# Gathering rows in quarters, a router by tile pairs and own banks for the first expert, in a hybrid encoder layer

## The reference

```
h      = rmsnorm(x1) * ffn_norm_g
logits = h @ w_router + b_router                  # 512 x 32
top 4 of 32 experts per token, softmax over the four -> gates
for each (token, expert) chosen:
    hu  = h @ w_gate_up[e] + b_gate_up[e]         # 1024 x 2048
    a   = min(hu[:1024], 7);  lin = clip(hu[1024:], -7, 7)
    act = a * sigmoid(1.702 a) * (lin + 1)
    y  += gate * (act @ w_down[e] + b_down[e])    # 1024 x 1024
out = rmsnorm(x1 + y) * final_norm_g
```

## Time and profile before

| | |
|---|---|
| three runs | 1348.56, 1343.34, 1342.54 us; median 1343.34 |
| profiled execution | 1343.47 us, span 1341.6 |
| PE busy | 1303.3 us (97%) |
| DVE / ACT / POOL busy | 508.4 / 205.2 / 246.7 us |
| bytes moved by DMA | 450.76 MB, mean 336 GB/s |
| mean granted TensorE clock | 0.988 |

### The profile page before, as it was taken

The page is one execution under the profiler, slowest core; times in us unless marked ns, Lnnn a source line. Parts: engine busy times, 40 slices in busy tenths (PEclk is TensorE's granted clock), DMA queues, the critical chain, the costliest instruction groups (busy, mean ns, idle before and its releaser), DMA issues.

```text
span 1341.6 us, 33185 instructions
## 1 busy us (share of the span) xinstructions
PE 1303.3 (97%) x14022; PEld 640.3 (48%) x14022; DVE 508.4 (38%) x895; ACT 205.2 (15%) x316; POOL 246.7 (18%) x252
## 2 busy tenths in 40 slices
PE   6999999998999999999999999999999999999996
PEld 6767778853444444444444444444444344444343
DVE  7676635542333332333222222222233333332235
ACT  5243333310010000001000000000010000000002
POOL 2145434100222211111111111111111111111100
PEclk9999998989999999999999999999999999999998
DMA  9222114678999999999999999999999999999984
GB/s 264 78 80 65 40 62 162 270 278 338 385 406 401 400 397 403 405 410 401 400 407 408 399 399 410 408 410 407 408 407 404 406 407 406 406 403 400 411 345 145
DMA packets 94606, 450.76 MB, mean 336 GB/s; under 512 B 12105, under 2 KB 36953, under 8 KB 45424
## 3 DMA queue, kind: packets, MB, share of 16 engines
q1 hardware_dynamic: 83280, 426.27, 79.6%
q0 software_dynamic: 8656, 19.48, 5.9%
q10 hardware_dynamic: 2640, 4.59, 0.9%
HBM read 440.06 MB, written 18.67 MB: 342 GB/s over the span
## 4 chain that ended last, share of the span: by engine, by line
PE 80%; DMA 9%; DVE 4%; SPq 3%; issue 2%; POOL 1%; ACT 1%; DVEq 0%; POOLq 0%; ACTq 0%
PE gu_bank L1630 40%; PE bank L1644 21%; DMA raw<-in_w_gate_up_dram 9%; PE bank L1391 4%; PE bank L1393 4%; PE bank L1392 4%; SPq L400 3%; PE bank L1618 2%; PE bank L1468 1%; PE bank L1482 1%; PE bank L1445 1%; PE bank L1647 1%; PE bank L1605 1%; DMA x_sb<-in_x_dram 0%; PE bank L1402 0%
## 5 line engine op out<-in xcount | busy, mean ns | idle before, releaser
L1630 PE MATMUL gu_bank<-raw,xT 128*32 128x512 f32 x3072 | 337.5, 592 | 4.7 <-DMA raw<-in_w_gate_up_dram 4.7
L1287 DVE TENSOR_TENSOR gate_in<-gu_bank,b_gu 128x768 f32<-128x768 f32 x32 | 30.6, 957 | 555.0 <-PE gu_bank L1630 542.0
L1630 PEld LDWEIGHTS gu_bank<-raw,xT 128*32 128x32 f32 x3072 | 100.5, 110 | 234.2 <-issue 211.9
L1644 PE MATMUL bank<-raw_a,aT 128*32 128x256 f32 x2232 | 166.8, 380 | 0.0
L1647 PE MATMUL bank<-raw_a,aT 128*32 128x256 f32 x744 | 166.4, 380 | 0.0
L1630 PE MATMUL gu_bank<-raw_c,xT 128*32 128x512 f32 x1488 | 165.5, 592 | 0.0
L589 POOL DMA_INDIRECT sum_rows<-y_out,scatter_list x31 | 45.6, 1472 | 418.0 <-ACT y_out L878 401.7
L1312 DVE STREAM_TRANSPOSE aT<-lin_in 128x192 f32<-128x192 f32 x128 | 68.0, 533 | 143.2 <-PE bank L1647 142.1
L1644 PEld LDWEIGHTS bank<-raw_a,aT 128*32 128x32 f32 x2232 | 88.8, 110 | 62.0
L864 ACT ACTIVATE xT<-bank 128x384 f32<-128x384 f32 x66 | 28.9, 489 | 551.9 <-PE bank L1618 541.4
L1630 PEld LDWEIGHTS gu_bank<-raw_c,xT 128*32 128x32 f32 x1488 | 49.8, 110 | 109.8 <-issue 103.5
(11 more groups left out here) (252 smaller groups left out, 1616.0 us busy)
## 6 DMA issues: line engine op xcount, KB each, us to landing
raw<-in_w_gate_up_dram SPq DMA_DIRECT2D x128, 1024.0 KB
raw_c<-in_w_gate_up_dram SPq DMA_DIRECT2D x62, 1024.0 KB
raw_a<-in_w_down_dram SPq DMA_DIRECT2D x62, 1024.0 KB
raw_b<-in_w_gate_up_dram SPq DMA_DIRECT2D x32, 1024.0 KB
raw_b<-in_w_down_dram SPq DMA_DIRECT2D x32, 1024.0 KB
raw_e<-in_w_gate_up_dram SPq DMA_DIRECT2D x31, 1024.0 KB
raw_d<-in_w_down_dram SPq DMA_DIRECT2D x31, 1024.0 KB
raw<-in_w_in_dram SPq DMA_DIRECT2D x24, 512.0 KB, 6.9
```

The costliest lines, as they stand in the source:

```text
L1287: dve.tensor_tensor(gate_in[:, :, :], gu_bank[:, :, 0:QUARTER], gate_b, ALU.add)
L1630: ins = pe.matmul(gu_bank[c * GROUP:(c + 1) * GROUP, r, :], xT[:, i, r * GROUP:(r + 1) * GROUP], w[:, c], start=first, stop=last)
L1644: pe.matmul(bank_[c * GROUP:(c + 1) * GROUP, cols], aT[:, k, c * GROUP:(c + 1) * GROUP], w[:, at:at + QUARTER], start=first and r % 2 == 0 ...
```

## The change

1. **Rows in quarters, turned and scaled by DVE.** xn_rows is read as 2048 rows of 1 KB. An expert's rows are gathered by three indirect DMAs (r = 0, 1, 2), partition 32c + t getting quarter c of the row of place 32r + t. In this layout DVE's transpose of 32 x 32 blocks makes xT directly, if partition p of a chunk holds row 8p + i of the weights; so the gate-up chunks (except the first expert's) are now read with rows 8p + i, one row of 8 KB in 64 KB. TensorE's transposes and ACT's copies go. The gain is multiplied in by DVE after the turn, and POOL's and DVE's multiplications of xn with a gain row go; xn_rows holds rows without gain. The row numbers (rows_q) are written by twelve small DVE instructions after the lists, and for the overflow by POOL after four more reads of the list.
2. **First expert.** Own banks (first_gu_bank) and own xT (first_xT, scaled by ACT and DVE on the way out of PSUM). The picking products run tile by tile, tile 0 while DVE chooses for the second pair. `sum_lists` stands behind the second chunk, with the counts in it. Gate-up of expert 1 doesn't wait for DVE to empty a bank.
3. **Router by pairs.** The router weights are now stationary, 32 columns to each of four column groups, and 64 tokens a group stream through: 32 products for a pair of tiles in place of 8 per tile. DVE turns the logits back with one transpose per pair and chooses two tiles at a time. The order of ACT's and DVE's steps around it is changed.
4. **Last channel tile** convolved by DVE, and one `sum_squares` moved ahead of the last `attend`.
5. The stores of x1 are issued by SP among the first expert's loads instead of by ACT.

```diff
-                sp.dma_start(raw_slot(m % RAW), w_gate_up[0, e, i * P:(i + 1) * P, :]).then_inc(w_loaded[m % RAW], 16)
+                sp.dma_start(raw_slot(m % RAW), w_gate_up[0, e].rearrange("(p i) n -> i p n", i=GU_CHUNKS)[i])\
+                  .then_inc(w_loaded[m % RAW], 16)
...
+            for i in range(GU_CHUNKS - 1):
+                load_first_gu(i)
+            for t in range(TT - 1):
+                store_x1(t)
+            load_first_gu(GU_CHUNKS - 1)
+            store_x1(TT - 1)
...
-            for t in range(TT - 1):
-                pool.wait_ge(xn_scaled, t + 1)
-                pool.tensor_tensor(xn[:, t, :], xn[:, t, :], g_ffn_row[:, :], ALU.mult).then_inc(xn_pool_ready, 1)
...
-                pool.wait_ge(got_turned, turned)
+                if not (isinstance(j, int) and j == 1):
+                    pool.wait_ge(x_turned, turned)
                 gather_rows()
...
             def gather_rows():
-                pool.indirect_dma_start(out=x_got[0:TILE, :], out_offset=None, in_=xn_rows,
-                                        in_offset=bass.IndirectOffsetOnAxis(ap=gather_list[0:TILE, 0:1], axis=0),
-                                        bounds_check=last_token, oob_is_err=False).then_inc(x_gathered, 16)
+                for r in range(GROUPS):
+                    pool.indirect_dma_start(out=x_got[:, r, :], out_offset=None, in_=xn_quarters,
+                                            in_offset=bass.IndirectOffsetOnAxis(ap=gather_list[:, r:r + 1], axis=0),
+                                            bounds_check=last_quarter, oob_is_err=False).then_inc(x_gathered, 16)
...
+                overflow = lists.rearrange("(r t j) w -> t r j w", r=GROUPS, t=GROUP)[:, :, E:PLACES, :]
+                for c in range(COLS):
+                    pool.dma_start(list_q[c * GROUP:(c + 1) * GROUP, :, :, :], overflow).then_inc(lists_held, 16)
...
             add_conv(0)
...
+            var_1(2)
             add_conv(3)
-            choose(0)
             take_x1T(2)
-            var_1(2)
-            choose(1)
             take_x1T(3)
             var_1(3)
-            choose(2)
-            choose(3)
+            logit_rows(0)
+            choose(0)
+            logit_rows(1)
+            pick_rows(0)
+            choose(1)
...
+            def turn_got(j, gathered):
+
+                dve.wait_ge(x_gathered, gathered)
+                dve.transpose(xT[:, :, :].rearrange("p k (r t) -> p k r t", r=GROUPS),
+                              x_got[:, :, :].rearrange("p r (f k) -> p k r f", k=KD)).then_inc(x_turned, 1)
+
+            def gain_got(j):
+
+                dve.wait_ge(x_turned, j)
+                dve.tensor_tensor(xT[:, :, :], xT[:, :, :], g_ffn_8[:, :].unsqueeze(2).to_broadcast([P, KD, TILE]),
+                                  ALU.mult).then_inc(x_gained, 1)
...
                 clamp(j, later(gu_chunk(n, GU_CHUNKS - 1) + 1, b, BODY * JOB))
+                turn_got(j + 1, gathered)
+                gain_got(turned)
                 gate(j)
...
+            def route(p):
+
+                pe.wait_ge(x1T_act_ready, 2 * p + 2)
+                pe.wait_ge(x1T_dve_ready, 2 * p + 2)
                 for k in range(KD):
-                    ins = pe.matmul(bank[2 * t][:, 0:E], x1T[:, k, t * P:(t + 1) * P], w_r[:, k, :],
-                                    start=k == 0, stop=k == KD - 1)
+                    tokens = x1T[:, k, 2 * p * P:2 * (p + 1) * P].rearrange("p (t n) -> p t n", t=2)
+                    for c in range(COLS):
+                        rows = slice(c * GROUP, (c + 1) * GROUP)
+                        ins = pe.matmul(bank[LOGIT_BANK[p]][rows, 0:2 * E], w_r[:, k, :], tokens[:, :, rows],
+                                        start=k == 0, stop=k == KD - 1)
...
+            turn_x1(2)
+            turn_x1(3)
+            route(0)
+            route(1)
+            rank_tiles(0)
+            pick_tile(0)
+            rank_tiles(1)
+            for t in range(1, TT):
+                pick_tile(t)
...
             def job(n, b=0):
                 j, turns = job_no(pe, n, b), turns_of(pe, b)
-                pe.wait_ge(gu_taken, j)
-                pe.wait_ge(xT_ready, j * 2 + 2)
+                if n == 1:
+                    pe.wait_ge(lists_taken, 2)
+                    pe.wait_ge(extra_ready, 1)
+                else:
+                    pe.wait_ge(gu_taken, j)
+                pe.wait_ge(x_gained, j)
                 for i in range(GU_CHUNKS):
                     m = gu_chunk(n, i)
                     gate_up(m, i, turns[m // RAW])
                 pe.wait_ge(aT_ready, fixed(pe, j * DN_CHUNKS))
-                transpose_got(j + 1)
```

More of the change, by code:

```diff
@@ L524, in _ @@
                     convolve(0)
-            for c in range(1, NC_):
+            for c in range(1, NC_ - 1):
                 convolve(c)
@@ L656, in _ @@
             pool.wait_ge(b_dn_loaded, dn_loads)
-            gathered = fixed(pool, end * 16)
+            gathered = fixed(pool, end * 16 * GROUPS)
             spread_dn()
@@ L879, in scale_y @@
                                scale=scatter_list[0:TILE, 1:2].bitcast(F32)).then_inc(y_ready, 1)
-            turned(0, xT, got_turned, xT_ready)
+            act.wait_ge(got_turned, 1)
+            for k in range(TT):
+                ins = act.activation(first_xT[:, k, :], bank[PICK_BANK][:, k * TILE:(k + 1) * TILE], ACT.Copy,
+                                     scale=g_ffn[:, k:k + 1])
+            ins.then_inc(first_xT_act_ready, 1)
             sigmoid(0)
@@ L1333, in _ @@
             spread_gu()
+            turn_got(1, 16 * GROUPS)
+            gain_got(1)
             clamp(0, GU_CHUNKS)
@@ L1595, in _ @@
-            for g in range(2):
-                for t in range(TT):
-                    if g == 0:
-                        pe.wait_ge(pick_ready, t + 1)
-                        if t < TT - 1:
-                            pe.wait_ge(xn_pool_ready, t + 1)
-                        else:
-                            pe.wait_ge(xn_dve_ready, 1)
+                pe.wait_ge(mask_ready, p + 1)
+                pe.matmul(cols, before[:, :], mask[:, first:first + 2, :].rearrange("p t e -> p (t e)"), start=True, stop=False)
@@ new lines, in rank_tiles, with pick_tile @@
+                for t in range(first):
+                    pe.matmul(cols, ones[:, :], mask[:, t, :].unsqueeze(1).to_broadcast([P, 2, E]), start=False, stop=False)
+                pe.matmul(bank[RANK_BANK][:, second * E:(second + 1) * E], ones[:, :], mask[:, first, :],
+                          start=False, stop=True).then_inc(rank_ready, 1)
+            def pick_tile(t):
+                pe.wait_ge(pick_ready, t + 1)
+                pe.wait_ge(xn_scaled, t + 1)
+                for g in range(2):
@@ L1615, in turn @@
-            def turn(src, done):
-                for g in range(2):
-                    for k in range(TT):
-                        ins = pe.transpose(bank[6 + g][:, k * TILE:(k + 1) * TILE],
-                                           src[0:TILE, (g * TT + k) * P:(g * TT + k + 1) * P],
-                                           ident[0:TILE, 0:TILE])
-                    ins.then_inc(done, 1)
-            def gate_up(m, i, loads):
+                    if t == TT - 1:
+                        ins.then_inc(got_turned, 1)
@@ L1686, in _ @@
                     job(n, b)
-            end, turns = fixed(pe, later(FIRST, count, BODY)), turns_of(pe, count)
-            turned_ = fixed(pe, later(2 * FIRST + 2, count, 2 * BODY))
-            pe.wait_ge(xT_ready, turned_)
+            turns = turns_of(pe, count)
             for i in range(DN_CHUNKS):
```

238 lines of the change are left out of this document (136 added, 102 removed).

## The result

The changed kernel takes 1306.32 us (median of 4 runs, 1304.07 to 1307.7) beside 1343.31: a ratio of 0.9721, 95% interval 0.97 to 0.9742. Forecast were 1335 and a range from 1322 to 1347. The direction was right; the gain is 37 us, where 8 were expected. Its profiled execution has a span of 1305.9 us.

The account below looks back on a forecast made before the run. The DMA engines were taken to bind the expert stage at about 32.9 us an expert against TensorE's 31.9. Sum: 1343.5 - 11.4 (start) - 1.6 (turn) + 3.1 (quarters) + 1.5 (overflow list) = 1335 us, range 1322 to 1347.

Parts of the forecast that it names:

- (e): Expert gather in quarters: 0.1 us more an expert, +3.1 us (bounds 0 and 8); overflow list reads +1.5 us.
- 32.9 us an expert: Expert stage: time the DMA engines need per expert, against TensorE's 31.9; taken to stay 32.9 to 33.0 after the change.
- (d): Each expert: turn on DVE takes 0.81 us off TensorE, DVE's work is covered; only the end gains, 1.6 us.
- the ring: Twelve weight chunks that hide the DMA engines' longer time per expert for some twenty experts, then are used up.
- (a): Before the experts: last channel on DVE, one TensorE order changed; recovers lowered clock, 1.5 us taken, 3 at best.
- (b): Before the first gate-up: router by tile pairs, gain off POOL and DVE; 5 us earlier, bounds 0 and 8.
- (c): First expert's own banks: refill pause shortened by 5.9 us, less 1.0 backlog; DMA run starts 11.4 us earlier with (a), (b).
- (f): Gate-up weights in another row order, 64 KB apart from partition to partition: taken as 0.
- B: Rival: more comes back, as quarters even out the slowest DMA engine or the start moves 15 us; 1323, chance 0.14.
- A: The forecast itself: DMA engines bind throughout, 1335, own range 1326 to 1342, chance 0.55.
- C: Rival: start moves little and quarters cost their upper bound; 1346, or 1343 with a start of 8 us; chance 0.20.
- D: Rival: weights read 64 KB apart come more slowly; 1359 at 4% slower; chance 0.11.

Follow-up runs that it names:

- e8: Kernel before, its gather of whole 4 KB rows spread over 128 partitions instead of 96 (the last 32 get no row): 1335.82 us, ratio 0.9924.
- e11: Changed kernel with eight extra TensorE transposes of a constant in each expert and the gathers issued behind the scatter: 1324.74 us, ratio 0.9855.
- e5: Changed kernel with POOL's three gathers for the next expert issued behind the scatter instead of ahead of it: 1305.42 us, ratio 0.9708.
- e2: Changed kernel with one gather of 96 whole 4 KB rows into 96 partitions instead of three of quarters into 128: 1322.74 us, ratio 0.9844.
- e14: Changed kernel with gate-up weights in old row order and one gather of 96 whole rows: 1323.36 us, ratio 0.984.
- e13: Kernel before, only its gate-up weights read in the new row order: 1345.76 us, ratio 1.0.
- e12: Changed kernel with expert 0's gate-up back in the bank of the others, lists and counts in banks 4 and 5: 1308.44 us, ratio 0.9731.
- e6: Changed kernel with gate-up weights in old row order and the gathers issued behind the scatter: 1303.46 us, ratio 0.9685.
- e10: e5 with the scatter of y also spread over 128 partitions, the last 32 writing nothing: 1323.02 us, ratio 0.9835.
- e7: e3 with its four gathers issued behind the scatter: 1326.69 us, ratio 0.9865.
- e9: e2 with its whole rows put to 128 partitions, of which the last 32 get none: 1314.49 us, ratio 0.9776.
- e1: Changed kernel with the gate-up weights of all experts read in their old row order: 1311.9 us, ratio 0.9759.
- e3: Changed kernel with four gathers of 1 KB quarters into 96 partitions each instead of three into 128: 1341.9 us, ratio 0.9985.

## Why the prediction was wrong

Three runs make a ledger of medians: the kernel before 1344.8, with the gather over 128 partitions 1335.8 (e8), with start and quarters too, TensorE's turn kept, 1324.7 (e11), without that turn 1305.4 (e5). That is -9.0, -11.1 and -19.3. The gather's new form, of which the 128 partitions are one part, was priced at +3.1, and the last edit at -1.6. The order of the edits matters: e2 has the start and TensorE's turn gone but the old gather, and takes 1322.7. With the start alone, not run by itself, 1344.8 - 11.1 = 1334 is the estimate. From there the gather alone gives 9 us (e11), the turn alone 11 (e2), and both together 28.

**The step that failed is (e), the gather, and with it the 32.9 us an expert that the sum carried over from before.** I asked what smaller pieces cost, gave bounds of 0 and +8, and so had no gain in the sum: the same bytes, and a share of 1.02 "with no idle time to win". The share counts time in which an engine has a packet in hand; the rate beside it, 346 instead of 424 GB/s in a window of four microseconds in each expert, was in the trace of before, and the prediction reads it only as means of 100 us (405, 406). At the rate between the dips, the weights' twelve chunks need 12.58 MB / 424 GB/s = 29.7 us. The remaining 3.2 of 32.86 us go with 64 gathered and 64 scattered rows, far more than their bytes. The term measures 31.7 to 31.84 and not 32.9 + 0.1.

With it my own sum comes out. Without the 3.1 for quarters it stands at 1332. The same seven late experts take 32.73 us before and 31.88 after, and thirty times that 0.85 is 25.5: 1306.5. By the four experts of the two chains (32.86 and 31.84) it would be 1301. So the sum is good to some 5 us, and that it meets 1306 so closely is luck. Another term was too small: reading the overflow list four more times, +1.5. The reads are issued at 450.58, and from 450 to 480 us the rate is 398, 279, 310, 377, 389 and 380 GB/s in steps of 5 us. Against 425 that is a loss of 4.9 us of transfers; the kernel before loses 1.6 in the same turn (465 to 490 us). So some 3.3 us are an estimate of it, which would put the sum at 1308; no run takes the reads out.

Not all of that 0.85 is the gather's form. e2 and e14, which have the old one, take 32.39 and 32.43 over the same seven experts, though their pieces are those of before and the order of the weights is excluded (e13, e14). So 0.5 us an expert belong to the form, the 16 us of e2, and 0.34 to something else, which over thirty experts are the 10 us by which e2 lies below 1332. By the packet records those 0.34 are mostly the weights' own packets between the gathers and scatters: 310 ns each in e2 and e14, 313 before. Of what differs within an expert, it is left that TensorE's turn is gone, or that the gather is issued at another place of the cycle; no run tells these apart.

**(d), TensorE's turn, -1.6.** The mechanism was as told (the loads bind earlier, the ring gives no more than they allow), and the covers held: no wait of TensorE for x or aT is in the chain. The size was wrong, in the main through the same number: had the loads needed 32.9, 0.8 us less on TensorE would have been of no use; at 31.7 it is TensorE that binds for some 14 experts, and the 0.95 us (the 0.81 and 0.14 around it) count fully up to 735 us and in part behind. e11 against e5 has 19.3 us for it. DVE is busy 12.0 us an expert where 12.9 were forecast (9.8 before); its turn takes 1.6 us and not 2.1.

**(a), (b), (c), the start, -11.4.** Right as a sum: first gate-up 6.2 us earlier for 6.5, gate-up of expert 1 9.5 for 10.6, and 11.1 between e8 and e11, where every later expert takes 31.91 in both. By the packet records the weights of the first three experts have landed at 350.3 us for 362.7, 12.4 earlier. How it is shared out was not tried but for the own banks, where e12 finds 2 us in place of 5.9, within the noise. For (a) the trace shows the cause at work: the granted clock of 0.82 in 200 to 210 us is 1.00 in the changed kernel. In (b) the sum is right, but the reading of one row is not: the instruction of 2.39 us is a comparison of 128x128, not the cast of 0.17 us that it is set beside.

**(f), the row order, 0.** Right: e13 and e6. The rule of the Trainium skill, "DMA: Bandwidth & Descriptors", section "Latency and other measured facts", on row pitches at large powers of two does not reach down to 64 KB in these runs (ratio 1.0, 0.9981 to 1.0019). The same row gives 214 GB/s as the full rate, so 207 at 512 KiB is hardly slower, and "about half" is said there of 4 and 8 MiB only.

**The rivals.** B had the right direction (quarters "even it out") with 5 us for it and a chance of 0.14; the "1306 were TensorE alone the bound" came out by luck: loads still bind from 751 us on. A and C held on to 32.9, and D had more. The general fault: a cost that I could not see was given bounds on one side of zero, and the number behind the whole sum was left out of the bounds.

## What to carry over

Where the transfers bind, read their rate in windows as short as one small transfer, not their share: a dip in the rate beside a full share is a cost that an edit can remove. Price the removed form of a transfer as well as the new one, and put the binding rate itself into the range. When TensorE and the DMA engines are within 1 us of each other, a saving on either alone is soon capped by the other: here 9 and 11 us alone, 28 together. And if TensorE pauses ahead of a loop's end with nothing to wait for, look at what POOL issues there and move it.

## What was not expected of the hardware

- *Shape of an indirect transfer.* 64 rows of 4 KB gathered into 96 partitions bring the rate down to 346 GB/s in a window of four microseconds; into 128 (32 of them without a row) it is 417 to 424 (e8), with three gathers of quarters into 128 424 to 426. In the scatter-add, 128 in place of 96 partitions cost 17.6 us more (e10). Quarters into 96 are no better than whole rows (32.62 us in e7, 32.39 in e2, over the same seven experts). The traces have each packet's duration; these are means from 1000 to 1240 us, in ns:

| | weights' 8 KB packets, during a gather | during a scatter | else | gather's 4 KB packets | scatter's 4 KB packets |
|---|---|---|---|---|---|
| before | 426 | 321 | 313 | 204 | 327 |
| e8, before, 128 partitions | 317 | 318 | 314 | 162 | 327 |
| e2, whole rows, 96 | 393 | 321 | 310 | 188 | 327 |
| e9, whole rows, 128 | 318 | 337 | 313 | 159 | 327 |
| e7, quarters, 96 | 350 | 321 | 311 | 173 | 327 |
| after, quarters, 128 | 309 | 321 | 309 | 159 | 327 |
| e10, after with gathers late and scatter over 128 | 318 | 321 | 316 | 160 | 349 |

  (Where quarters are gathered, one packet can hold four pieces of 1 KB.) So a gather into 96 partitions does not add much work of its own: for some 2.2 us it makes the packets of both kinds slower, the weights' by a third. And a row of the scatter-add holds an engine for 327 ns, twice as long as a gathered row, whatever the gather's form. Why 96 partitions do this no run shows; how the rows fall to the single engines is not in these traces.
- *Pauses of TensorE with nothing to wait for.* Three or four gathers in the last 5 us of a loop iteration cost TensorE 0.64 us an iteration (e1), up to 2.1 (e3), and nothing when they stand in the middle of it (e6, e7, e11). The changed kernel has its gathers at the same place without a gap, and e1 differs from it only in the order of the weights: it stands near the edge, and what tips it is open. Nor is the way from the gathers to TensorE shown. It is not the loading of code by a transfer: from 400 to 1200 us, 25 iterations of e1, the queues for instructions moved one packet in all:

```profile
q14 instruction: 1, 0.01, 0.0%
```

  The Trainium skill, "Runtime: NRT & Kernel Launch", section "Instruction fetch mechanics", warns of branches whose target has to be fetched by DMA first; here the branch back is in each iteration, with and without the gap, and by that row no such fetch stands behind it.
